# Second layer norm of a hybrid encoder: the statistics of tiles 0 and 1 on ScalarE, and three changes of order

## The reference

```python
def layer_norm(x, g, b):
    mu = jnp.mean(xf, axis=-1, keepdims=True)
    var = jnp.mean(jnp.square(xf - mu), axis=-1, keepdims=True)
    return ((xf - mu) * lax.rsqrt(var + LN_EPS) * g + b)
...
h = layer_norm(x, ln_in_g, ln_in_b)
for l in range(DEPTH):
    ...
    h = layer_norm(DN_ALPHA * h + mix @ w_out[l], ln1_g[l], ln1_b[l])
    ffn = jnp.square(jax.nn.relu(h @ w1[l])) @ w2[l]
    h = layer_norm(DN_ALPHA * h + ffn, ln2_g[l], ln2_b[l])
```

## Time and profile before

| | before |
|---|---|
| median of 3 runs | 1079.35 us (1078.64 to 1080.85) |
| the profiled execution | 1078.98 us |
| its span, first to last instruction | 1077.2 us |
| mean granted TensorE clock | 0.998 of full speed |
| TensorE busy, matmuls | 1056.3 us, 98% of the span |
| VectorE busy | 794.8 us, 74% |
| ScalarE busy | 506.5 us, 47% |
| DMA | 105.52 MB, mean 98 GB/s |

### The profile page before, as it was taken

How to read it: one execution, slowest core, us unless ns; L and a number is a source line. 1 busy time by engine, 2 the same in 40 slices (tenths; PEclk the granted TensorE clock), 3 DMA queues, 4 the chain that set the end, 5 groups by cost and what they waited for, 6 DMA issues and landing times.

```text
span 1077.2 us, 15569 instructions
## 1 busy us (share of the span) xinstructions
PE 1056.3 (98%) x5310; PEld 896.5 (83%) x5310; DVE 794.8 (74%) x1108; ACT 506.5 (47%) x754; POOL 91.2 (8%) x84
## 2 busy tenths in 40 slices
PE   7999999999999999999999999999999999999996
PEld 6888889998888888888778888899888888888884
DVE  7855886968757757758977568777794784784788
ACT  3432666365355355355323347653743643643650
POOL 5200222100000000000002003221000000000001
PEclk9999999999999999999999999999999999999999
DMA  8422013030521521421333410310334134134122
GB/s 286 157 108 87 2 60 119 1 124 25 211 79 40 183 90 39 169 105 61 113 109 152 156 40 20 116 43 12 115 116 158 40 117 157 39 103 170 40 78 79
DMA packets 17380, 105.52 MB, mean 98 GB/s; under 512 B 2016, under 2 KB 2704, under 8 KB 5792
## 3 DMA queue, kind: packets, MB, share of 16 engines
q1 hardware_dynamic: 15984, 98.70, 25.2%
q0 software_dynamic: 1184, 5.86, 1.7%
q10 hardware_dynamic: 144, 0.07, 0.0%
HBM read 101.49 MB, written 2.10 MB: 96 GB/s over the span
## 4 chain that ended last, share of the span: by engine, by line
PE 92%; DVE 5%; issue 2%; ACT 0%; DMA 0%; DVEq 0%
PE bank L446 18%; PE bank L448 18%; PE bank L447 18%; PE bank L750 8%; PE bank L752 8%; PE bank L751 8%; PE bank L696 4%; PE bank L682 2%; PE bank L593 1%; PE bank L455 1%; PE bank L594 1%; DVE x L1539 1%; DVE w_lo L1142 1%; PE bank L527 1%; PE bank L606 1%
## 5 line engine op out<-in xcount | busy, mean ns | idle before, releaser
L446 PE MATMUL bank<-h_hi,w_hi 128*128 128x512 f32 (+1 forms) x704 | 260.8, 370 | 0.3
L447 PE MATMUL bank<-h_lo,w_hi 128*128 128x512 f32 (+1 forms) x704 | 260.3, 370 | 0.0
L448 PE MATMUL bank<-h_hi,w_lo 128*128 128x512 f32 (+1 forms) x704 | 260.3, 370 | 0.0
L750 PE MATMUL bank<-w_hi,hid_hi 128*128 128x512 f32 x448 | 174.6, 390 | 1.6 <-DVE x L1539 1.6
L751 PE MATMUL bank<-w_lo,hid_hi 128*128 128x512 f32 x448 | 174.3, 389 | 0.0
L752 PE MATMUL bank<-w_hi,hid_lo 128*128 128x512 f32 x448 | 174.3, 389 | 0.0
L1142 DVE TENSOR_TENSOR w_lo<-w_raw,w_hi 128x2048 fp32r<-128x2048 f32 x62 | 141.8, 2288 | 36.8 <-ACT w_hi L867 30.0
L446 PEld LDWEIGHTS bank<-h_hi,w_hi 128*128 128x128 f32 x704 | 132.6, 188 | 23.4 <-issue 1.1
L447 PEld LDWEIGHTS bank<-h_lo,w_hi 128*128 128x128 f32 x704 | 132.7, 188 | 22.4
L448 PEld LDWEIGHTS bank<-h_hi,w_lo 128*128 128x128 f32 x704 | 132.6, 188 | 22.4
L867 ACT CAST w_hi<-w_raw 128x2048 fp32r<-128x2048 f32 x56 | 107.1, 1913 | 78.9 <-PE bank L752 56.4
(11 more groups left out here) (167 smaller groups left out, 1634.0 us busy)
## 6 DMA issues: line engine op xcount, KB each, us to landing
w_raw<-in_weights SPq DMA_DIRECT2D x63, 1024.0 KB, 4.8
w_third<-in_weights SPq DMA_DIRECT2D x23, 1024.0 KB, 4.8
rows<-in_rows POOLq DMA_DIRECT2D x4, 1024.0 KB, 5.0
w_raw<-in_weights SPq DMA_DIRECT2D x4, 512.0 KB, 7.6
out_h<-x SPq DMA_DIRECT2D x8, 256.0 KB, 2.0
x<-in_x SPq DMA_DIRECT2D x3, 512.0 KB, 9.9
dft<-in_dft SPq DMA_DIRECT2D x2, 512.0 KB, 6.8
qk_gain<-in_qk_gain POOLq DMA_DIRECT2D x3, 192.0 KB, 3.3
```

Source lines behind the costliest of these rows:

```text
L446: pe.matmul(dst, s_hi, m_hi, start=first, stop=False)
L447: pe.matmul(dst, s_hi, m_lo, start=False, stop=False)
L448: return pe.matmul(dst, s_lo, m_hi, start=False, stop=last)
L750: pe.matmul(bank[dst + t][:], s_hi, m_hi, start=start, stop=False, skip_group_check=goes_on)
```

## The change

The last norm of each layer takes the mean and variance of tiles 0 and 1 from ScalarE: a copy of the 1024 columns with a sum, the negated mean, and a square of the centred columns with a sum (`row_moments`); VectorE adds epsilon to that sum (`variance_of_squares`) and centres with the negated mean. Tiles 2 and 3 keep VectorE's statistics, now called where they stand in the list. Addition 9 goes ahead of the norm, and the additions, splits and steps of the norm have a new order at the boundary, the same list in both layers with the If parts. ScalarE's splits of the next layer's blocks 0 and 1 stand behind the first and the second tile's passes. TensorE turns tile 0 of the next layer before the last 3 matmuls of T4's first run instead of before the run. In the attention an "s" item goes between the two row maxima. At the start tile 1 is loaded ahead of the second half of block 0, all its statistics are taken before `h_lo` of tile 0, and GpSimd takes two parts instead of three ahead of tile 1's power. The first norm of a layer is the same with other counts (`normalise_first`).

The diff, cut to its core:

```diff
-    stats=16, moments=8, var_ready=8, rstd=8, centred=16, normed=16, rows=32,
+    stats=12, moments=6, row_sum=2, neg_mean=2, row_square=2, var_ready=8, rstd=8, centred=16, normed=16, rows=32,
...
-            def load_weights(b):
-                c = slice(0, BLOCK // 2)
-                sp.dma_start(w_raw[:, b, c], w_in[b, :, c]).then_inc(w_half_landed[b], 16)
-                c = slice(BLOCK // 2, BLOCK)
-                sp.dma_start(w_raw[:, b, c], w_in[b, :, c]).then_inc(w_landed[b], 16)
+            def load_weights(b, half):
+                c = slice(half * BLOCK // 2, (half + 1) * BLOCK // 2)
+                sp.dma_start(w_raw[:, b, c], w_in[b, :, c]).then_inc((w_half_landed, w_landed)[half][b], 16)
...
-            load_weights(0)
+            load_weights(0, 0)
             load_tile(1)
-            load_weights(1)
+            load_weights(0, 1)
+            load_weights(1, 0)
+            load_weights(1, 1)
...
-                                if last_chunk and b == T4 and (t, kt) == (0, 0):
+                                if last_chunk and b == T4 and (t, kt) == (0, 3):
                                     with pe.If(l < DEPTH - 1):
                                         turn(l + 1, 0)
...
+                def row_moments(t):
+
...
+                    if t == 0:
+                        wait(act, l, "hidden_lo", 12 * CHUNKS)
+                    else:
+                        wait(act, l, "row_square", t)
+                    wait(act, l, "added", 32 + CHUNK_ADDS * (CHUNKS - 1) + 8 + t + 1)
+                    act.activation(junk, x[:, t, :], ACT.Copy, accum_out=row_sum[:, t:t + 1]).then_inc(sems["row_sum"], 1)
+                    wait(act, l, "row_sum", t + 1)
+                    act.activation(neg_mean[:, t:t + 1], row_sum[:, t:t + 1], ACT.Copy, scale=-1.0 / D_MODEL).then_inc(sems["neg_mean"], 1)
+                    wait(act, l, "neg_mean", t + 1)
+                    act.activation(junk, x[:, t, :], ACT.Square, bias=neg_mean[:, t:t + 1], accum_out=row_square[:, t:t + 1])\
+                       .then_inc(sems["row_square"], 1)
+
+                def split_parts(b, raw):
+                    wait(act, l + 1, "products", NEXT_RELEASED[b] - CHUNK_G)
+                    for part in range(PARTS):
+                        split_part(l + 1, b, part, raw)
+
+                row_moments(0)
                 with act.If(l < DEPTH - 1):
-
-                    for b in range(2):
-                        if b == 0:
-                            act.wait_ge(third_landed, (l + 1) * (48 * CHUNKS))
-                        else:
-                            act.wait_ge(w_landed[1], (l + 1) * (16 * LANDED[1]) + 16)
-                        wait(act, l + 1, "products", NEXT_RELEASED[b] - CHUNK_G)
-                        for part in range(PARTS):
-                            split_part(l + 1, b, part, w_third[:] if b == 0 else w_raw[:, 1, :])
+                    act.wait_ge(third_landed, (l + 1) * (48 * CHUNKS))
+                    split_parts(0, w_third[:])
+                row_moments(1)
+                with act.If(l < DEPTH - 1):
+                    act.wait_ge(w_landed[1], (l + 1) * (16 * LANDED[1]) + 16)
+                    split_parts(1, w_raw[:, 1, :])
                     stream_high(l + 1, 0, 0, 0)
                     stream_high(l + 1, 0, 0, 1)
...
-            def variance(k, t, stats_done):
-
...
+            def variance(t, stats_done, moments_done, eps=LN_EPS / ALPHA ** 2):
+
+                counted = dve.to_reg(stats_done)
                 dve.wait_ge(x_landed[t] if t else x_half_landed[1], 16)
                 dve.wait_ge(sems["stats"], counted)
                 dve.bn_aggr(moments[:, t, :], bn[:, t, :, :].rearrange("p a b -> p (a b)")).then_inc(sems["moments"], 1)
-                dve.wait_ge(sems["moments"], 4 * k + (t + 1))
-                eps = LN_EPS / ALPHA ** 2 if not isinstance(k, int) or k else LN_EPS
+                dve.wait_ge(sems["moments"], moments_done)
                 dve.tensor_scalar(var_eps[:, t:t + 1], moments[:, t, 1:2], eps, None, ALU.add).then_inc(sems["var_ready"], 1)
 
-            def centre(k, t):
-
-                dve.wait_ge(sems["moments"], 4 * k + (t + 1))
+            def variance_of_squares(l, t):
+
+                wait(dve, l, "row_square", t + 1)
+                dve.tensor_scalar(var_eps[:, t:t + 1], row_square[:, t:t + 1], 1.0 / D_MODEL, LN_EPS / ALPHA ** 2, ALU.mult, ALU.add)\
+                   .then_inc(sems["var_ready"], 1)
...
+            def centre(k, t, moments_done=None):
+
...
+                    if moments_done is None:
+                        dve.scalar_tensor_tensor(out=x[:, t, c], in0=x[:, t, c], scalar=neg_mean[:, t:t + 1], in1=rows[:, c],
+                                                 op0=ALU.add, op1=ALU.mult).then_inc(sems["centred"], 1)
...
-            variance(0, 0, 2)
+            variance(0, 2, 1, LN_EPS)
             first_norm(0)
-            dve.wait_ge(x_landed[1], 16)
-            row_stats(1, 0)
+            input_stats(1)
             stream_low(0, 0, 0)
-            row_stats(1, 1)
-            variance(0, 1, 4)
             first_norm(1)
...
+
+                        if u % 2 == 0:
+                            for k in sides_of(p):
+                                if SIDE[k][0] == "s":
+                                    side(k)
                     for k in sides_of(p):
-                        side(k)
+                        if SIDE[k][0] == "w":
+                            side(k)
...
                         dve.wait_ge(sems["added"], l * PER_LAYER["added"] + c * CHUNK_ADDS + (32 if before is None else 32 + before + t + 1))
                         xs = x[:, tile + t, half * BANK:(half + 1) * BANK]
                         dve.tensor_tensor(xs, bank[dst + t][:], xs, ALU.add).then_inc(sems["added"], 1)
-                        if last and p in (3, 4, 5, 6):
-                            wait(dve, l, "added", 32 + CHUNK_ADDS * (CHUNKS - 1) + n + 1)
-                            row_stats(tile + t, half)
+
+                    def stats_of(tile, half, after):
+                        wait(dve, l, "added", 32 + CHUNK_ADDS * (CHUNKS - 1) + after + 1)
+                        row_stats(tile, half)
+
+                    def variance_of_stats(t):
+                        variance(t, l * 12 + (16 + 2 * (t - 2) + 2), l * 6 + (8 + t - 1))
...
                     add(6)
                     add(7)
                     add(8)
+                    add(9)
                     if not last:
-                        add(9)
...
                     k = 2 * l + 2
-                    variance(k, 0, 3)
-                    normalise(k, 0)
-                    add(9)
-                    variance(k, 1, 4)
+                    variance_of_squares(l, 0)
+                    centre(k, 0)
+                    scale(k, 0)
                     add(10)
+                    stats_of(2, 1, 10)
+                    variance_of_squares(l, 1)
+                    centre(k, 1)
+                    add(11)
+                    scale(k, 1)
+                    with dve.If(l < DEPTH - 1):
+                        stream_low(l + 1, 0, 0)
+                    add(12)
+                    stats_of(2, 0, 12)
+                    variance_of_stats(2)
                     with dve.If(l < DEPTH - 1):
                         for part in range(PARTS):
                             split_part(l + 1, 0, part)
-                    centre(k, 1)
-                    add(11)
+                        stream_low(l + 1, 0, 1)
+                    centre(k, 2, l * 6 + (8 + 1))
                     with dve.If(l < DEPTH - 1):
-                        stream_low(l + 1, 0, 0)
-                    scale(k, 1)
-                    add(12)
-                    variance(k, 2, 7)
-                    centre(k, 2)
-                    with dve.If(l < DEPTH - 1):
-                        stream_low(l + 1, 0, 1)
                         for part in range(PARTS):
                             split_part(l + 1, 1, part)
+                    stats_of(3, 1, 11)
                     scale(k, 2)
                     add(13)
-                    variance(k, 3, 8)
-                    centre(k, 3)
+                    stats_of(3, 0, 13)
+                    variance_of_stats(3)
+                    centre(k, 3, l * 6 + (8 + 2))
                     with dve.If(l < DEPTH - 1):
                         stream_low(l + 1, 0, 2)
                     scale(k, 3)
...
-            for part in range(PARTS - 1):
+            for part in range(2):
                 split_low_part(0, 0, part)
             layer_norm_rstd(0, 1, 2)
-            split_low_part(0, 0, PARTS - 1)
+            for part in range(2, PARTS):
+                split_low_part(0, 0, part)
```

More of the change, by code:

```diff
@@ L279, in build @@
         moments, _ = place("moments", [P, TOK, 2])
+        row_sum, _ = place("row_sum", [P, 2])
+        neg_mean, _ = place("neg_mean", [P, 2])
+        row_square, _ = place("row_square", [P, 2])
```

(5 more changed lines are left out.)

24 lines of the change are left out of this document (14 added, 10 removed).

## The result

The kernel after takes 1072.76 us (median of 5 runs, 1072.30 to 1073.33), the kernel before in the same comparison 1078.89 (5 runs, 1078.55 to 1080.85): a ratio of 0.9943 with an interval of 0.9933 to 0.9954.

The account below looks back on a forecast made before the run. With TensorE busy 98%, only its idle time could be won: start 1.1, pair 3 1.1, boundary 0.8 and tail 1.3 make 4.3 off 1078.98, or 1075.0 us on the median's level; range 1073.2 to 1077.5.

Parts of the forecast that it names:

- the boundary: Between layers 1 and 2: T4 ends 2.0 us sooner, a new stall leaves a gain of 0.8; bounds -0.5 and 2.0.
- the 1.48 us of "issue" before the next layer stays: Between T4's end and layer 2: TensorE's idle 1.48 us at the layer loop's jump was taken as unchanged.
- rival 4: In T4: the moved If stalls TensorE at the jump's price of 1.48 us, tail's gain gone, 1076.3; chance 0.05.
- The new wait on `h_lo` of tile 2: Early in layer 2: VectorE's longer list makes TensorE stall 1.1 us, plus 0.1 for starting again.
- The start: First norm: tile 1 loaded sooner, its centring and turn 1.1 us sooner; gain 1.1, between 0 and 1.5.
- rival 3: At the start: tile 1 lands no sooner, gain 0.2 in place of 1.1, time 1075.9; chance 0.06.
- Pair 3: Attention, both layers: mean square goes between two row maxima on VectorE; 0.57 us a layer, 1.1 together, lower bound 0.6.
- The passes: ScalarE's copy, negation and square for a tile's statistics: 2.7 us a tile, between 2.4 and 3.9.
- Rivals 2 and 5: 2: ScalarE's passes take 3.9 us, 1077.5, chance 0.08. 5: VectorE parks on ScalarE's sums, slower, 1080.5 at 4.7 us, 0.03.
- The tail: End of layer 2, VectorE's list is the path: gain 1.3 us; 0.1 with passes of 3.9, 1.4 with 2.4.
- Rival 1: At the boundary: VectorE catches up, h_lo of tile 2 is in time, the 2.0 us stays whole, 1073.8; chance 0.12.
- Rival 6: Mid-layer: loads of the next blocks hold TensorE, little more than the tail's 1.3 is left, 1077.8; chance 0.05.

## Why the prediction was right or wrong

**The step that failed** is in the boundary: "the 1.48 us of 'issue' before the next layer stays". I took it for a fixed price of the loop's jump, in the sum and in rival 4. The jump takes longer than that (4.07 us before, 3.51 after), and the 1.48 was the part of it that T4's matmuls did not cover: with TensorE's last wait in T4 taken away, the branch starts 3.40 us ahead of T4's last matmul in place of 2.48, no load lies beside it, and nothing is left of the 1.48. The forecast of 4.3, this 1.48 and the 0.31 of chance at the start make 6.1. By the clock the miss is small: the same kernel once more gave 1073.26, just inside the range. The step is wrong all the same, as the idle time is gone in both profiles.

**The boundary otherwise** came as laid out. T4's last matmul stands 19.11 us behind additions 4 and 5 (536.50 less 517.39) for 21.16 before (540.54 less 519.38): 2.05 sooner, forecast 2.0. TensorE's timeline of the kernel before:

```profile
540.54 0.39 PE L752 MATMUL bank<-w_hi,hid_lo 128*128 128x512 f32 x1
```

The new wait on `h_lo` of tile 2 is 1.0, and the stretch behind the layer's start is 1.29 longer than pair 3 alone makes it (505.91 for 504.62); forecast 1.1 + 0.1. From `h_lo` of tile 1 to that of tile 2 it is 10.02 us (540.06 to 550.08), forecast 10.1. So the boundary gave 2.2 in place of 0.8.

What I had credited wrongly, without harm to the sum, is the cause of the sooner T4: I wrote of statistics leaving VectorE, and the run with the order alone shows that the order is enough.

**The start**: 1.12 from the first matmul to the turn, forecast 1.1; the load of tile 1 was there by 8.98, forecast 9.1, so rival 3 falls. That the turn stands 1.43 sooner on the clock is chance of the run for the rest.

**Pair 3**: 0.56 and 0.59, forecast 0.57 each.

**The passes**: 2.66 us, forecast 2.7, and the square pass 1.15, from the row of 1024 columns. Rivals 2 and 5 fall; the run with longer passes shows the slope that the rivals gave for the tail: 1.10 us later for passes of 3.75 us in place of 2.66.

**The tail**: 1.29, forecast 1.3, with 2.03 us of VectorE's wait ahead of addition 9, for the tenth product, which I had put at 2.0.

**Rival 1** gave 1073.8, the nearest time, for a reason that did not happen, so its nearness is luck: `h_lo` of tile 2 is late by what I had said. **Rival 4** falls by the run with the turn put back. **Rival 6** falls: the gains arrive at the end.

## What to carry to other kernels

An idle stretch without a releaser ahead of a loop's next turn is not a constant: look up the branch's own record, what the engine waited for last before it, and what the DMA engines did then; taking away a late wait, or moving a bulk load off the branch, may win that stretch on top of the wait itself. When a list is reordered and work is moved to another engine in one change, run the order alone: here it made all of the boundary's gain, and the moved work paid only where the engine's list is the end of the program. Compare stretches between marks within one execution, since the start alone moved by up to 1.2 us from one execution to the next.

## What the runs showed of the hardware that was not expected

- The branch back to the start of the layer loop took TensorE's sequencer 3.35 to 4.11 us in thirteen profiles, and 5.95 with 1 MB loaded beside it; at the loop's end, where it is not taken, 0.08. The jump back in the chunk loop of the kernel before (line 820, at 370.66) took 0.24, with no 16 KB packet on queue 8 between 357.4 and 465.6.
- A load of 1 MB that TensorE does not wait for cost it 2.43 us at a branch of its program.
- The first matmul behind the loop's branch stood 2.5 to 3.3 us behind the start of one 16 KB instruction packet in all 14 profiles, whether 0 or 2.43 us of that was idle time.
- The wait on `h_lo` of tile 2 was 0.98 to 1.01 us in the kernel after and with 0.7, 1.0 and 2.4 us of gap ahead of the layer, since its chain begins with TensorE's own turn: a wait that does not shrink when TensorE comes later.
